# A two-layer decoder trunk: the layers written out one after the other in one block instead of a loop with a barrier

## What is computed

```python
for layer in range(2):
    shift1, scale1, gate1, shift2, scale2, gate2 = split(silu(c) @ ada_w[layer] + ada_b[layer])
    h = rms_norm(x, g_mix) * (1 + scale1) + shift1
    # one input projection feeds three mixers: Mamba-2 SSD, latent attention, block-sparse attention
    x = x + gate1 * (mixers(h @ w_in) @ w_out)
    h = rms_norm(x, g_ffn) * (1 + scale2) + shift2
    # 16 experts, each token goes to 2 of them with weights w1, w2
    x = x + gate2 * (w1 * expert[e1](h) + w2 * expert[e2](h))
```

## Time and profile before

| what | value |
|---|---|
| median of 3 timed runs | 1477.59 us (1475.14 to 1477.91) |
| span of the profiled execution, first to last instruction | 1470.7 us |
| PE, DVE, ACT, POOL busy | 90%, 79%, 50%, 16% of the span |
| mean granted TensorE clock | 0.955 of full speed |

### The profile page before, as it was taken

How to read it: one execution, slowest core, us unless ns; L and a number is a source line. 1 busy time by engine, 2 the same in 40 slices (tenths; PEclk the granted TensorE clock), 3 DMA queues, 4 the chain that set the end, 5 groups by cost and what they waited for, 6 DMA issues and landing times. The chain is left out here.

```text
span 1470.7 us, 17413 instructions
## 1 busy us (share of the span) xinstructions
PE 1323.4 (90%) x6467; PEld 1048.2 (71%) x6467; DVE 1162.9 (79%) x1379; ACT 739.2 (50%) x969; POOL 239.1 (16%) x296
## 2 busy tenths in 40 slices
PE   6799987889989999999949998878998999999993
PEld 2577865667878888888747777566777788888871
DVE  3569856885579999999855988488656999999986
ACT  1334333562437777777413343447223877777750
POOL 0100125431011000000121012345110100000002
PEclk9899988989999999999979999898999999999996
DMA  9676621433579999999558483133347999999965
GB/s 357 240 261 223 203 90 59 143 100 131 218 283 361 413 411 416 407 402 376 196 180 294 170 270 120 58 115 115 130 152 287 362 404 407 413 404 407 403 225 197
DMA packets 96788, 382.29 MB, mean 260 GB/s; under 512 B 6009, under 2 KB 8807, under 8 KB 86968
## 3 DMA queue, kind: packets, MB, share of 16 engines
q1 hardware_dynamic: 73144, 311.50, 55.9%
q0 software_dynamic: 15232, 55.63, 9.7%
q10 hardware_dynamic: 8320, 13.96, 2.7%
HBM read 348.25 MB, written 32.82 MB: 259 GB/s over the span
## 5 line engine op out<-in xcount | busy, mean ns | idle before, releaser
L1274 PE MATMUL ps<-mod_rounded,work_rounded 128*128 128x512 f32 x340 | 136.9, 403 | 1.1 <-DVE work_rounded L2281 1.1
L1276 PE MATMUL ps<-mod_rounded,work_rounded 128*128 128x512 f32 x340 | 134.4, 395 | 0.0
L1275 PE MATMUL ps<-ring_rounded,work_rounded 128*128 128x512 f32 x288 | 113.7, 395 | 0.0
L1735 DVE SCALAR_TENSOR_TENSOR gain<-ring,csil,gain 128x512 f32<-128x512 f32 x134 | 104.3, 778 | 3.3
L2140 DVE TENSOR_TENSOR ring_rounded<-ring,mod_rounded 128x2048 fp32r<-128x2048 f32 (+1 forms) x54 | 102.8, 1929 | 1.4
L1275 PE MATMUL ps<-work_rounded 128*128 128x512 f32 x256 | 101.0, 395 | 0.0
L2140 DVE TENSOR_TENSOR work_rounded<-work,mod_rounded 128x2048 fp32r<-128x2048 f32 (+1 forms) x48 | 91.3, 1930 | 9.6 <-ACT mod_rounded L1635 8.4
L927 PE MATMUL ps<-ring_rounded,actT_rounded 128*128 128x512 f32 (+1 forms) x256 | 93.4, 365 | 0.0
L2512 POOL DMA_INDIRECT work<-ffn_rows,slot_idx x34 | 42.0, 1234 | 302.9 <-PE ps L1260 270.1
L1635 ACT ACTIVATE mod_rounded<-ring 128x2048 fp32r<-128x2048 f32 (+1 forms) x54 | 85.9, 1625 | 0.0
L1276 PE MATMUL ps<-actT_rounded,work_rounded 128*128 128x512 f32 x204 | 80.4, 394 | 0.0
(11 more groups left out here) (370 smaller groups left out, 3635.9 us busy)
## 6 DMA issues: line engine op xcount, KB each, us to landing
ring<-in_ada_w SPq DMA_DIRECT2D x38, 1024.0 KB, 5.2
ring<-in_moe_w_gate SPq DMA_DIRECT2D x18, 2048.0 KB, 10.1
ring<-in_moe_w_up SPq DMA_DIRECT2D x18, 2048.0 KB, 10.4
ring<-in_moe_w_down SPq DMA_DIRECT2D x18, 2048.0 KB
work<-in_moe_w_up SPq DMA_DIRECT2D x16, 2048.0 KB, 10.6
work<-in_moe_w_down SPq DMA_DIRECT2D x16, 2048.0 KB, 11.6
work<-in_moe_w_gate SPq DMA_DIRECT2D x16, 2048.0 KB, 10.3
expert_rows<-work POOLq DMA_DIRECT2D x32, 512.0 KB, 7.7
```

Of the source, the lines that this page charges most:

```text
L1274: pe.matmul(ps[j][:, :], xl, hi, start=k == 0, stop=False)
L1275: pe.matmul(ps[j][:, :], xh, lo, start=False, stop=False)
L1276: mm = pe.matmul(ps[j][:, :], xh, hi, start=False, stop=k == KD - 1)
L1735: add(v.scalar_tensor_tensor(acc, w, csil[:, k:k + 1], acc, ALU.mult, ALU.add))
```

## The change

Each engine's program is now `def layer(L)`, called for L = 0 and L = 1 in one block. No barrier, no loop and no clearing of semaphores stands between; they count on, and `at(L, sem, n)` is the count n in layer L. With L known, parts are left out where they aren't needed: in the last layer the modulation blocks 8 to 11 with their loads, sums and rows (`sums(L)` is 8 there), the loading and splitting of the next layer's first weights, its gain and its shift and scale; in layer 1 the writing of zeros, and its wait; in layer 0 the `If` with the tiny memsets. The tile sums, the chosen rows and the normed rows of the next layer stand in one order by token tile (`TOKEN_ORDER`, `added`, `chosen_added`). PE runs 36 `keep_warm` in place of 8 before the first turning of layer 1. The output is written at the end of the same block.

```diff
+TOKEN_ORDER = [(0, 0), (0, 1), (1, 0), (1, 1), (0, 2), (1, 2), (0, 3), (1, 3)]
+def at(layer, sem_, n):
+    return sem_, n + layer * per_layer[sem_.num]
+def sums(layer):
+    return NADA if layer + 1 < DEPTH else NEARLY
-with nc.Fori(0, DEPTH) as L:
+# on every engine:
+for L in range(DEPTH):
+    layer(L)
 # PE, start of a layer
-keep_warm(8)
+if L:
+    pe.wait_ge(*at(L - 1, x_added, 1))
+    keep_warm(36, bank=0)
+else:
+    keep_warm(8)
 to_columns(0)
-keep_warm(8)
+keep_warm(8, bank=0)
+if L:
+    pe.wait_ge(*at(L, in_w_lo, 0))
+    pe.wait_ge(*at(L - 1, x_added, 2 * T))
 # DVE, start of a layer
+def added(L, t):
+    for b in range(2):
+        v.wait_ge(ov_pe[L], TOKEN_ORDER.index((b, t)) + 1)
+        add_by_token(0, b, t).then_inc(x_added, 1)
-chosen_added(0, 0)
-chosen_added(0, 1)
+if L:
+    added(L - 1, 0)
+    added(L - 1, 1)
+    chosen_added(L - 1, 0, 0)
+    chosen_added(L - 1, 0, 1)
 for t in range(T):
-    v.wait_ge(cdn, t + 1)
+    if L:
+        v.wait_ge(*at(L - 1, cdn, t + 1))
+        if t + 2 < T:
+            added(L - 1, t + 2)
     ...
 def late_adds(n):
+    if sums(L) == NEARLY:
+        return
 # DVE, end of a layer
+more = L + 1 < DEPTH
+if more:
+    v.memset(prow[:], 0.0).then_inc(pads, 1)
+    first_in_lo(v, 0, at(L, in_w_hi, 2 * (len(IN_ORDER) - 1))[1])
 y_out(e, e % 2, halves=(0,))
-first_in_lo(v, 1, 2 * (len(IN_ORDER) - 1))
+if more:
+    first_in_lo(v, 1, at(L, in_w_hi, 2 * (len(IN_ORDER) - 1))[1])
 y_out(e, e % 2, halves=(1,))
-v.wait_ge(next_b, 16)
-mix_gain(v)
+if more:
+    v.wait_ge(*at(L, next_b, 16))
+    mix_gain(v, 16 * (L + 1))
-for b in range(2):
-    for t in range(T):
-        v.wait_ge(cb_ps, T * b + t + 1)
-        add_by_token(0, b, t)
 # POOL, end of a layer
 g.wait_ge(*at(L, yw[0], 8 * NE))
 g.wait_ge(*at(L, yw[1], 8 * NE))
-g.sem_clear(range(cg[0].num, cg[-1].num + 1))
-g.dma_reset(range(first, cg[-1].num + 1))
 gather_chosen()
-nc.all_engine_barrier(sems_to_clear=range(first, last + 1))
 # DVE, behind both layers
+for t in range(T):
+    added(DEPTH - 1, t)
+    chosen_added(DEPTH - 1, t, 0)
+    chosen_added(DEPTH - 1, t, 1)
```

More of the change, by code:

```diff
@@ L447, in trunk @@
[L447 to L457 removed]
+    acc_ps = sem("acc_in_psum", 32)
@@ new lines, in trunk @@
+    sel_dn = sem("slot_selectors_done", 2)
+    tab_ps = sem("slot_table_in_psum", 1)
+    tab_sb = sem("slot_table_out", 3)
+    gat = [sem(f"tokens_gathered{n}", (144, 128)[n]) for n in range(2)]
+    xt_ps = sem("expert_tokens_transposed", 34)
+    xt_ev = sem("expert_tokens_columns_out", 34)
+    xl_dn = sem("expert_tokens_low_done", 34)
+    w_hi = sem("weights_high_done", 68)
+    w_lo = sem("weights_low_done", 68)
+    d_hi = sem("down_weights_high_done", 51)
+    d_lo = sem("down_weights_low_done", 51)
@@ new lines, in trunk @@
+    hl_lo = sem("hidden_columns_low_done", 17)
+    gu_ps = sem("gate_up_in_psum", 34)
+    sil = sem("gate_silu_done", 17)
+    hid_dn = sem("hidden_done", 17)
+    ht_ps = sem("hidden_transposed", 17)
+    ht_ev = sem("hidden_columns_out", 17)
+    y_ps = sem("expert_out_in_psum", 34)
+    y_ev = sem("expert_out_scaled", 34)
+    yw = [sem(f"expert_out_stored{n}", 128) for n in range(2)]
+    turn, ov_w, ov_g, ov_pe, ov_act, ov_dve = (
+        [sem(f"further_{what}_of_layer{n}") for n in range(DEPTH)]
+        for what in ("turn", "weights_loaded", "tokens_gathered", "matmul_step", "scalar_step", "vector_step"))
@@ L460, in trunk @@
+    TURN_PE, TURN_ACT, TURN_DVE = 2 * T + 4, 3, 3
+    x_added = sem("x_added_by_token", 8)
+    cdn = sem("token_tile_combined", 4)
+    cg = [sem(f"choices_gathered{n}", 32) for n in range(T)]
+    all_sems = range(sems[0].num, sems[-1].num + 1)
+    assert len(all_sems) == len(sems)
     start_bufs = [slots[3], slots[4], actT[:, :, :].rearrange("p a b -> p (a b)"), slots[2]]
@@ L626, in ada_block @@
     def ada_block(m, layer):
-        return (layer, 4 + m) if m < NEARLY else ((layer + 1) % DEPTH, m - NEARLY)
+        return (layer, 4 + m) if m < NEARLY else (layer + 1, m - NEARLY)
     in_width = [min(512, NIN - 512 * b) for b in range(6)]
@@ L1637, in _ @@
-                x_squares(0, True)
-                for t in range(T):
-                    if t < T - 1:
-                        x_squares(t + 1, True)
-                    columns_out(T, t)
-                    if t == T - 2:
-                        weights_hi(0, 0, (0,), first=True)
-                    a.wait_ge(rt_ps, t + 1)
-                    if t:
-                        a.wait_ge(rt_rows, t)
-                    a.activation(rt_cols, ps[4][0:NE, P * t:P * t + P], ACT.Exp, scale=-1.0).then_inc(rt_ex, 1)
```

3482 lines of the change are left out of this document (1723 added, 1759 removed).

## The result

| | before | changed |
|---|---|---|
| median of 4 runs | 1477.75 us | 1440.09 us (1437.67 to 1441.93) |
| ratio of the runs | | 0.976, 95% interval 0.9741 to 0.9779 |
| span of the profiled execution | 1470.7 us | 1439.8 us |
| its own time | not given | 1441.93 us |
| mean granted TensorE clock | 0.955 | 0.963 |

The kernel is faster by 37.7 us in the medians, 33 to 38 by the interval. The forecast was 1442 with a range of 1433 to 1456.

The account below looks back on a forecast made before the run. Experts, with PE and DVE always busy, can't move; the seam waits for gathers, and DVE is busiest in most attention stretches. Gains 0.7 + 13.4 + 11.7 + 9.5 = 35.3 take span 1470.7 to 1435.4; plus 6.9, forecast 1442 us, range 1433 to 1456.

Parts of the forecast that it names:

- Start of layer 0: Layer 0's beginning: without the `If` and the memsets ACT's first squares start about 0.7 us earlier; -0.7 us.
- The seam: Between the layers: a wait for gathers, then some 5 us of barrier and branch, would go; -13.4 us.
- The 0.8 taken off for late rows: Layer 1's start: two late tile sums delay DVE's next rows, so PE waits about 1.3 us instead of 0.5.
- Attention: Layer 1's attention: 27.6 us of late modulation work leaves DVE, the busiest engine of most stretches; -11.7 us.
- the replay from n = 20 on: Attention steps n = 20 to 31 worked through without late adds; running gain from -3.3 to -10.7 us.
- The first rival: Attention: late adds were cover, ACT's splits and POOL's norms hold it; gives 2 of 11.7 us, total 1452; chance 0.15.
- Behind the attention: Output products after layer 1's attention: one modulation sum less on PE, 1.0 us.
- The end: Last layer's end: DVE skips splits and next scale, gathers go out earlier, rows are added tile by tile; -9.5 us.
- the bound of -11.5: End of the last layer: the gain if DVE alone set the pace, against the forecast -9.5 us.
- The 6.9 us from span to median: Whole kernel: the median stands 6.9 us above the profiled span, so a span of 1435.4 became 1442.3 us.
- the rival: Seam: DVE's chosen adds hold up three of POOL's gathers and the root; +3 us, total 1445; chance 0.13.
- Instruction supply: Whole kernel: rival that longer straight code makes instructions late; twelve stops, 37 us, eat the gain, sixteen give 1492; chance 0.04.

Follow-up runs that it names:

- e3: Changed kernel, with layer 1 again waiting for all tile sums and gathers, and 8 warming products; sums to projection 28.02 us, median 4.4 us above a1's.
- e7: Changed kernel, with DVE making only 16 of 2048 columns of a low part of layer 1's first weights; both gather issues take 0.98 us.
- a1: The changed kernel run again, unedited; median 1443.72 us, ratio 0.9772 to the kernel before.
- e2: Changed kernel with the late modulation kept in the last layer; head 5 to last product 44.7 us against 39.1 in a1, median 7.5 us above a1's.
- e8: Changed kernel, with DVE instead of ACT making layer 1's last three high parts and its first low part at n = 23; head 7 to last 21.18 us.
- e10: Changed kernel, with DVE in the last layer adding all tile sums, then waiting for all gathers, then adding rows; the end 2.7 us longer.
- e11: Changed kernel with the edits of e6 and e9 together; median 1434.22 us, ratio 0.9708.
- e5: Changed kernel, with ACT making only 16 of 2048 columns of layer 1's last three high parts of the output weights; median 1435.51 us.
- e6: Changed kernel, with DVE's first low part of layer 1's output weights moved from n = 19 to n = 23; 4.2 us less from head 5 to last product.
- e9: Changed kernel with warming products on PE in two pauses, 9 before the last expert tile's second half and 5 behind the attention; median 1442.95 us.

## Why the prediction was right, by its steps

The time was right, and so was the seam's mechanism, to 1 us. The attention and the clock behind it were sized wrong, and an offset that was wrong too made up for them: that the total came within 2 us is luck.

**Start of layer 0.** -0.7 shows as long as the clocks agree: DVE's instructions at 347 us stand 0.70 earlier. At 721 us PE is 1.35 us ahead, and by the first tile sum that is gone, in the slow stretch behind the pause.

**The seam.** Forecast 19.8 us from sums to projection (750.9 - 731.1), measured 19.18 and 18.88. e3 shows that 8 to 9 of the 14.7 us were the wait for all gathers, as "a wait for gathers whose first tile had long landed" had it. I took the gathers to move 1.1 us ahead; the first moved 2.3 ahead in the changed kernel's trace but was held 2.1 us longer by DVE's split, which e7 shows, so that the second stood at 732.76, forecast at 732.3. The 0.8 taken off for late rows came to nothing. Behind the first row PE waits for one row only, 0.43 us where it waited 0.47 before, and from the first projection to the first turning of a head it is 139.3 to 139.4 us in a1, e2, e7, e8, e10 and e11 against 139.50 before. What the changed kernel's own trace lost there, 1.4 us, is the stretch at the lower clock at 773 us.

**Attention.** The step that failed is the replay from n = 20 on. It took the durations of the trace of before, with the late adds left out, and let PE and ACT set the pace as if DVE's absence slowed nobody. What it missed stood in two places. ACT's three high parts sit in one row with the exponentials, and e5 shows 6.2 us for them, 3.0 of them at equal clock. DVE's low part now falls beside POOL's multiplication for head 6, and e6 shows 0.9 us for it at equal clock and 1.7 by the clock, which e11 repeats. PE's clock was below full in all three stretches; the replay had added 1.0 us for that. The first rival named ACT's splits and POOL's norms as the holders: it was right about who holds, and wrong that only 2 of the 11.7 us would come. Measured are 8.0 us in the trace, 1.5 of them ahead of head 5 and 6.5 behind, and 7.0 by e2 against a1. Of the 2.3 us from head 5 to head 6 the adds gave little: e2, which has them, took 10.68 us there at a clock of 1.00, where the kernel before took 12.50 at 0.73. The attention lasted 39.3 us from head 5 on, between the 36 forecast and the 42 that would have refuted it.

**Behind the attention.** "1.0 us of PE in an unbroken row" became 1.9 us more, by the lower clock: e8's trace has a mean of 1.00 there, as before, and took 399.47 us against 399.67. In e9, without the stretches behind the pauses of 1.4 and 2.5 us, it was 400.05. What the modulation sum alone gave is not shown.

**The end.** -11.6 and not -9.5 (-10.5 by the second trace of before). The mis-sized term is the 1.5 us for the last store that no longer shares its way. From its issue to its landing it took 6.4 us before and 2.9 now, 3.5 less. So the rows are there when DVE wants them, and DVE alone sets the pace, which was the bound of -11.5. From PE's last tile sum to the end it is 14.1 us, less than the 15 to 18 expected.

**From the trace to the median.** The terms sum to 35.3, the trace gives 30.9: 4.4 too much. The 6.9 us from span to median should have been 2.1: 4.8 too much. The two cancel by luck, and 1442 is nearer to 1440.09 than its parts deserve. Against the medians, with the kernel before at 1475 to 1478, the gain is 32 to 38 us.

**What holds POOL.** The Trainium skill (SBUF — State Buffer, section SBUF: two separate sides) says that the pair of ports that VectorE and GpSimd share goes to whichever instruction starts first, for its whole length, and that a VectorE instruction with two SBUF inputs claims it only against a GpSimd instruction that reads SBUF. The traces agree for POOL's multiplication, which reads SBUF: 0.84 us alone, 2.85 when it starts 0.13 us behind DVE's subtraction. Gather issues, which read their row numbers (`pos_i`) from SBUF, are held in the traces too, and end 0.86 us behind the split. Beside a chosen add it is less: the last issue of the end took 1.85 us, and 0.94 in e10, where it stood beside tile sums, which have one input in PSUM. As the rival had it this would have cost 3 us in the seam; it cost none, because PE's warming products end at the same time anyway.

**Instruction supply.** No engine fell behind in straight code: DVE's instructions that stood at 822 to 942 us before stand 13.10 to 13.12 us earlier throughout, and those of the experts from 1164 to 1407 us 20.77 to 20.81 us.

## What to carry to other kernels

Where a barrier stands between stages, ask what lands last behind it and what the first consumer needs: here 8 to 9 of 14.7 us were rows of tiles not yet needed. Where work is taken from the busiest engine, redo the order of the others around it: each long instruction that was hidden behind that engine's work (ACT's 1.9 us copies, DVE's 2.3 us subtraction beside POOL) is now in somebody's way. Moving one of them by four steps gave 2.6 us in two traces and 4.2 in the better of them. And where the clock changes between two traces, compare stretches of equal clock before a cause is named. Before a sum is set against a single profiled execution, find out how far that execution lies from the median.

## What the runs showed of the hardware that was not expected

A gather's issue on POOL beside a DVE instruction with two SBUF inputs (128x2048, 2.28 us) took up to 3.10 us where it took 0.98 alone.

The same pause of PE, 2.5 us long ahead of the last expert products, was followed by full clock in both traces of the kernel before, in both layers, and by some 3 us at the lower level (0.50, 1.2 GHz) in the changed one: in layer 0 in all ten traces without warming products there, in layer 1 in seven of them, with the same products ahead of it. What PE did before the pause does not tell the two apart, and no experiment did. Warming products in the pause removed the stretch, and others can stand elsewhere: e9 had one at 433 us that the other traces lack. The time of one and the same kernel spreads over 9 to 11 us, and the slower runs have the lower mean clock: the kernel before took 1468.7 us at 0.957 and 1479.63 at 0.947.
